# RWKV solve on 32x32 blocks in four array tiles, and six modulation blocks of each layer at another place

## The chip, the cores and the metric

The kernel runs on one core of one Trainium2 chip. The metric is device time in microseconds (us). Three runs of the kernel before took 1097.0, 1099.38 and 1100.24 us; the median is 1099.38.

## What is computed

The program is a decoder trunk of two layers on 256 positions and 1024 channels in float32. Each layer modulates a normed input with vectors `mod = silu(c) @ w_mod + b_mod`, projects it, and mixes it in three branches (a gated linear recurrence, differential attention, RWKV-7), which are merged by sigmoid gates; a gated MLP follows. The change touches two things: how the RWKV branch is solved, and when the modulation vectors are summed. For each of 8 heads RWKV is this recurrence:

```python
state = (state * w_t[:, :, None, :] + sa[..., None] * b_t[:, :, None, :]
         + v_t[..., None] * k_t[:, :, None, :])      # sa = state a_t
return state, jnp.einsum("bhvk,bhk->bhv", state, r_t)
```

The kernel cuts the 256 positions into 4 chunks of 64. Inside a chunk the recurrence is a linear system with a unit triangular 64x64 matrix, one for each of the 8 heads and 4 chunks, so 32 matrices in a layer. Between the chunks a state is handed on (the state chain).

## The kernel before, in words

Every engine runs a program of its own, in order, and the engines wait on each other's semaphores. Nothing plans the order: it is written out by hand.

**TensorE (PE).** Large products take weights in two parts (high and low, fp32r) and make three matmuls of each (`passes`, L1784 to L1786, and `token_unit`, L1973 to L1979). The gates and the merge weights of the branches are such products with 512 columns, cut into 36 weight chunks per layer. They depend on little, so they serve as filling: `fill(point)` issues the next `FILL[point]` of these matmuls wherever PE would otherwise wait for another engine. What is not used as filling is issued afterwards in one piece (`fill_some(12 * NCHUNK)`).

**The solve** (`STEPS`, `solve_steps`). It inverts the 32 triangular matrices by doubling: blocks of 2, then 4, 8, 16, 32 and 64, so five levels behind the first. The products are plain float32, and each shows as two matmul records and two weight loads in the trace. `chunk_products` (L2075) makes the matrices: K against KK ("ak"), KK against AB ("n") and AB against KK ("nt", the transposed form), each 32 products of 64x64. In them four array tiles are in use, since both the 64 rows of the head's half and the 64 columns of the chunk's half change. A level is two steps, "m" and "x", each done for `par` 0 and 1: `block_products` (L2084) makes 16 products of 64x64 per `par`, on the two diagonal tiles of the array. VectorE reads each result with a mask ("m", L1519) or adds it ("x", L1525), and after "x" it turns both matrices in blocks of 32 (L1529). Behind each step PE issues 8 matmuls of filling (6 behind the last). `Mm`, `Nm`, `Tm` and `TTm` hold 16 blocks of 64x64 each. The first level of all, with blocks of two, is made by `blocks_of_two` (L1491, L1515) on identities that ScalarE writes (L874, L875).

**Behind the solve** come the products with its result (L2125, L2132), the read products (L2075, L2149) and the state chain over 4 chunks: PE (L2166 to L2180) and VectorE (L1544 to L1554) in turn, with 4 matmuls of filling at a time, and one weight chunk's low part (L1350) by VectorE after each state.

**Modulation.** w_mod is read in blocks of 128x1024 (512 KB). VectorE adds each block to an accumulator (`mod_block`, L1112 for the first of 8 and L1115 for the others); `mod_beside(n)` takes the next n blocks at the place where it stands. Eight blocks make a vector, which PE then sums over partitions (`mod_sum`, L1743: a wait on `mod_used` for the eighth block, then 8 small matmuls), and VectorE reads (`mod_vector`). GpSimd (POOL) issues the loads into two buffers (`mod_blocks`, L560), each when the block two before it was used; between them it does the low parts of nine weight chunks (L586) and the state factors and merges (L594 to L607). SP issues the weight loads `pair(g)` of 1 MB into four buffers. ScalarE makes the high parts (`act_chunks`, L778).

## Time and profile before

| what | value |
|---|---|
| three runs | 1097.0 to 1100.24 us, median 1099.38 |
| the profiled execution | 1098.47 us |
| its span, first to last instruction | 1096.7 us |
| granted TensorE clock, mean | 0.992 |
| PE busy, VectorE busy, ScalarE busy | 98%, 77%, 53% of the span |
| DMA | 214.81 MB, mean 196 GB/s |

The span is 1.8 us shorter than the execution's own time, and this execution is 0.9 us below the median. PE is TensorE with its matmuls, PEld its weight loads. "Busy" of PE counts pipelined matmuls, so it says that PE is occupied and not that it is at its peak. "issue" as a releaser is time in which nothing that the profile shows held the engine. A clock of 1.0 is 2.4 GHz and one of 0.5 is 1.2 GHz.

### The profile page before, as it was taken

How to read it: one execution, taken by the hardware profiler on the slowest of the kernel's cores; microseconds unless marked ns; L12 is line 12 of the kernel's file. 1: busy time of each engine (PE TensorE's matmuls, PEld its weight loads, DVE VectorE, ACT ScalarE, POOL GpSimd, SP SyncE). 2: the span in 40 equal slices, each digit the busy share in tenths (PEclk: the TensorE clock that was granted, in tenths of full speed). 3: DMA queues.
4: the chain of work that ended last, by engine and by line, in shares of the span. 5: the costliest groups of instructions: out<-in, count | busy, mean ns of one | idle time of the engine just before them, and what ended most of it. 6: DMA issues, size and time to landing. Idle time of an engine off the chain costs nothing.

```text
span 1096.7 us, 23323 instructions
## 1 busy us (share of the span) xinstructions
PE 1075.3 (98%) x9660; PEld 989.9 (90%) x9660; DVE 845.3 (77%) x1245; ACT 582.7 (53%) x894; POOL 125.8 (11%) x142
## 2 busy tenths in 40 slices
PE   8999999899999999999999999999999999999997
PEld 7889988787789999999989999878887999999997
DVE  4798998686578798987758899977755878888763
ACT  2266567532364666663355575683227466666533
POOL 0100000056002000001120000002640200000001
PEclk8999999999999999999999999999999999999999
DMA  9946455443156567667854546361615465555651
GB/s 378 342 172 217 178 172 225 180 154 139 42 208 235 188 233 245 218 234 292 311 189 167 206 157 223 144 229 60 232 59 192 154 244 184 186 191 191 222 201 39
DMA packets 41460, 214.81 MB, mean 196 GB/s; under 512 B 7936, under 2 KB 8320, under 8 KB 22048
## 3 DMA queue, kind: packets, MB, share of 16 engines
q1 hardware_dynamic: 29856, 171.65, 42.8%
q0 software_dynamic: 11520, 41.95, 10.8%
q8 instruction: 64, 1.05, 0.4%
q14 instruction: 20, 0.16, 0.0%
HBM read 212.01 MB, written 1.05 MB: 194 GB/s over the span
## 4 chain that ended last, share of the span: by engine, by line
PE 93%; DVE 4%; DMA 2%; issue 1%; ACT 1%; DVEq 0%; ACTq 0%
PE ps L1786 18%; PE ps L1784 17%; PE ps L1785 17%; PE ps L1975 6%; PE ps L1979 6%; PE ps L1973 6%; PE ps L1804 5%; PE ps L2084 2%; DMA mring<-wmod_dram 2%; PE ps L1743 1%; DVE macc L1115 1%; PE ps L2256 1%; PE ps L2075 1%; PE ps L1761 1%; PE ps L2000 1%
## 5 line engine op out<-in xcount | busy, mean ns | idle before, releaser
L965 ACT ACTIVATE WH<-ring 128x1024 fp32r<-128x1024 f32 x144 | 151.9, 1060 | 164.9 <-PE ps L1786 157.2
L1634 DVE TENSOR_TENSOR WLO<-ring,WH 128x1024 fp32r<-128x1024 f32 x144 | 175.8, 1234 | 70.0 <-ACT WH L965 70.0
L1786 PE MATMUL ps<-HH,WLO 128*128 128x256 f32 x736 | 208.1, 283 | 0.0
L1785 PE MATMUL ps<-HL,WH 128*128 128x256 f32 x736 | 206.6, 281 | 0.0
L1784 PE MATMUL ps<-HH,WH 128*128 128x256 f32 x736 | 205.0, 279 | 0.0
L1786 PEld LDWEIGHTS ps<-HH,WLO 128*128 128x128 f32 x736 | 138.7, 188 | 0.0
L1784 PEld LDWEIGHTS ps<-HH,WH 128*128 128x128 f32 x736 | 138.5, 188 | 0.0
L1785 PEld LDWEIGHTS ps<-HL,WH 128*128 128x128 f32 x736 | 138.0, 188 | 0.0
L560 POOL DMA_DIRECT2D mring<-wmod_dram x80 | 43.4, 542 | 763.2 <-DVE macc L1115 456.5
L1115 DVE SCALAR_TENSOR_TENSOR macc<-mring,sm,macc 128x1024 f32<-128x1024 f32 x70 | 96.5, 1378 | 16.4 <-DMA mring<-wmod_dram 14.4
L1786 PE MATMUL ps<-GH,WLO 128*128 128x256 f32 x384 | 108.3, 282 | 0.0
L1784 PE MATMUL ps<-GH,WH 128*128 128x256 f32 x384 | 108.2, 282 | 0.0
L1785 PE MATMUL ps<-GL,WH 128*128 128x256 f32 x384 | 107.9, 281 | 0.0
L1786 PE MATMUL ps<-HG,RLO 128*128 128x256 f32 x384 | 107.9, 281 | 0.0
L1662 DVE SCALAR_TENSOR_TENSOR TK<-ps,PR,TK 128x255 f32<-128x255 f32 x192 | 79.1, 475 | 0.0
L1979 PE MATMUL ps<-RLO,HG 128*128 128x512 f32 x192 | 77.7, 405 | 0.0
L1786 PEld LDWEIGHTS ps<-GH,WLO 128*128 128x128 f32 x384 | 73.7, 192 | 0.0
L1786 PEld LDWEIGHTS ps<-HG,RLO 128*128 128x128 f32 x384 | 72.5, 189 | 0.0
L1785 PEld LDWEIGHTS ps<-GL,WH 128*128 128x128 f32 x384 | 72.2, 188 | 0.0
L1784 PEld LDWEIGHTS ps<-GH,WH 128*128 128x128 f32 x384 | 72.1, 188 | 0.0
L778 ACT ACTIVATE WC<-ring 128x1024 fp32r<-128x1024 f32 x36 | 37.8, 1055 | 62.3 <-PE ps L1975 33.1
L1784 PE MATMUL ps<-HG,WCR 128*128 128x256 f32 x208 | 58.8, 283 | 0.0
(404 smaller groups left out, 2552.7 us busy)
## 6 DMA issues: line engine op xcount, KB each, us to landing
ring<-wmain_dram SPq DMA_DIRECT2D x150, 1024.0 KB, 4.9
mring<-wmod_dram POOLq DMA_DIRECT2D x80, 512.0 KB, 5.0
G<-wmod_dram SPq DMA_DIRECT2D x3, 1024.0 KB, 10.0
R<-wmod_dram SPq DMA_DIRECT2D x3, 1024.0 KB, 17.7
TK<-wmod_dram SPq DMA_DIRECT2D x2, 1024.0 KB, 20.5
X<-x_t_dram SPq DMA_DIRECT2D x1, 1024.0 KB, 5.8
y_dram<-H SPq DMA_DIRECT2D x4, 256.0 KB, 2.1
SW<-small_dram SPq DMA_DIRECT2D x1, 512.0 KB, 13.6
```

The lines of the kernel that those rows point to most:

```text
L560: pool.dma_start(mring[:, n % 2, :], wmod[mod_row(n)]).then_inc(s_m[n % 2], 16)
L965: A(WH[:, n % 2, part], ring[:, b, part], ACT.Copy).then_inc(hi_ready, 1)
L1115: V.scalar_tensor_tensor(macc[:, u % 2, :], block, sm[:, CSIL + kt:CSIL + kt + 1], macc[:, u % 2, :], ALU.mult, ALU.add).then_inc(mod_used, 1)
L1634: V.tensor_tensor(WLO[:, n % 2, part], ring[:, b, part], WH[:, n % 2, part].bitcast(F32), ALU.subtract).then_inc(lo_ready, 1)
L1662: ins = V.scalar_tensor_tensor(UB[:, q % 2, t, d:S], duo(b)[:, t, 0:S - d], PR[:, l, bass.ds(j + (COL["fw"] + 48 * (2 - d)), 1)], UB[:, q ...
L1784: MM(out, w_high[:, at], high, start=start, stop=False, skip_group_check=True)
L1785: MM(out, w_high[:, at], low, start=False, stop=False, skip_group_check=True)
L1786: return MM(out, w_low[:, at], high, start=False, stop=stop, skip_group_check=True)
L1804: last = MM(ps[:, g % 4, m * S:(m + 1) * S], w_of(g, m, i), rhs[:, i, :], start=(i == 0), stop=(i == KT - 1))
L1973: MM(ps[:, b, :], high[:, tk], w_high, start=(k == 0), stop=False, skip_group_check=True)
L1975: i = MM(ps[:, b, :], low[:, tk], w_high, start=False, stop=False, skip_group_check=True)
L1979: i = MM(ps[:, b, :], high[:, tk], w_low, start=False, stop=(k == nk - 1), skip_group_check=True)
```

## The change

- The first four levels (blocks up to 32) work on the 32x32 diagonal blocks alone. A step has 32 products of 32x32 per `par` where it had 16 of 64x64, on four diagonal array tiles where it used two. The operands `Nn`, `Tn`, `TTn` and `Mn` have 256 elements per partition and `par` where they had 512, so VectorE's reads, adds and turns are half as long.
- The last level ("m" and "x" with v = 4) joins two 32x32 halves: "m" has 16 products per `par` on two tiles, "x" 32 on four, half of which only copy a block with the identity. VectorE copies the results, and one more operation writes the left half of `TTm`.
- "n" is made as 64 products with 64 rows and 32 columns (`narrow_products`), "nt" falls away, and in its place come 32 such products ("off"), which ScalarE reads.
- `blocks_of_two` falls away; two masks, two adds of the identity and two turns on VectorE take its place, and ScalarE no longer writes identities.
- Six calls' worth of modulation blocks leave the projections of each layer. One goes behind the solve, and five into the state chain. In layer 0 the eighth block of the first vector stands behind weight chunk 16, ahead of `mod_vector(6 * l + 2)`. GpSimd's loads are shifted to fit.
- SP loads the masks in 12 transfers where it needed 4.
- `FILL` is as before.

```diff
-(M_LOW, M_UP, M_UPI, M_L1, M_U1, M_U2, M_U4, M_U8, M_U16, M_U32, M_ID) = range(11)
...
+(M_UP, M_UPI, M_U32) = range(3)
+(N_LOW, N_UP, N_UPI, N_L1, N_U1, N_U2, N_U4, N_U8, N_U16, N_ID) = range(10)
+Q = 32
...
-LEVELS = [M_U2, M_U4, M_U8, M_U16, M_U32]
+LEVELS = [N_U2, N_U4, N_U8, N_U16, None]
+LAST = len(LEVELS) - 1
...
-    steps = [("ak", 0, 0, 4), ("ak", 1, 0, 5), ("n", 0, 0, 6), ("n", 1, 0, 7), ("nt", 0, 0, 4), ("nt", 1, 0, 5)]
+    steps = [("ak", 0, 0, 4), ("ak", 1, 0, 5), ("n", 0, 0, 6), ("n", 1, 0, 7), ("off", 0, 0, 4), ("off", 1, 0, 5)]
...
+def tiles_used(kind, v):
+
+    return {"ak": 1, "n": 4, "off": 2, "m": 2 if v == LAST else 4, "x": 4}[kind]
+
+
+SOLVED = [int(n) for n in np.cumsum([tiles_used(k, v) for k, _, v, _ in STEPS])]
...
-        TTm, Nm, Tm, Mm = mats(0, 4), mats(4, 8), mats(8, 12), mats(12, 16)
+        def narrow_mats(a):
+            return R[:, a:a + 2, :].rearrange("p a b -> p (a b)").rearrange("p (g m s) -> p g m s", g=2, s=Q)
+
+        TTm, Mm = mats(0, 4), mats(12, 16)
+        Nn, No, Tn, TTn, Mn = [narrow_mats(a) for a in (4, 6, 8, 10, 12)]
...
@@ -521,9 +555,14 @@
                 if l == 0:
                     for half in (0, 1):
                         rows = slice(64 * half, 64 * half + 64)
-                        sp.dma_start(CM[rows, 0:NCOMP - 1, :], consts[rows, AT_MASKS:AT_MASKS + (NCOMP - 1) * P]
+                        sp.dma_start(CM[rows, M_UP:M_UPI + 1, :], consts[rows, AT_UP:AT_UP + 2 * P]
                                      .rearrange("p (n s) -> p n s", s=P)[:, :, 64 * half:64 * half + 64]).then_inc(s_masks, 16)
-                        sp.dma_start(CM[rows, M_ID, :], consts[rows, 64 * half:64 * half + 64]).then_inc(s_masks, 16)
+                        sp.dma_start(CM[rows, M_U32, :], consts[rows, AT_U32 + 64 * half:AT_U32 + 64 * half + 64]).then_inc(s_masks, 16)
+                    for g in range(4):
+                        rows = slice(Q * g, Q * g + Q)
+                        sp.dma_start(CN[rows, N_LOW:N_ID, :], consts[rows, AT_MASKS:AT_MASKS + N_ID * P]
+                                     .rearrange("p (n s) -> p n s", s=P)[:, :, Q * g:Q * g + Q]).then_inc(s_masks, 16)
+                        sp.dma_start(CN[rows, N_ID, :], consts[rows, Q * g:Q * g + Q]).then_inc(s_masks, 16)
...
-                m1 = m0 + 16
-                mod_blocks(m0 + 2, m1)
...
                     if i < 7:
-                        mod_blocks(m1 + i, m1 + i + 1)
+                        mod_blocks(m0 + 10 + i, m0 + 11 + i)
...
-                mod_blocks(m1 + 7, m1 + 8)
+                mod_blocks(m0 + 17, m0 + 24)
...
-                act.wait_ge(s_masks, 64)
-                A(TTm.rearrange("p g m s -> p (g m) s"), over(small_mask(M_ID), 16), ACT.Copy).then_inc(i_ready, 1)
-                A(Tm.rearrange("p g m s -> p (g m) s"), over(small_mask(M_ID), 16), ACT.Copy).then_inc(i_ready, 1)
...
+                for par in range(2):
+                    act.wait_ge(t_mm, SOLVED[-1] * l + products_until("off", par))
+                    A(No[:, par], narrow(4 + par), ACT.Copy).then_inc(off_ready, 1)
...
-                mod_beside(2)
...
-                if l:
-                    mod_beside(2)
...
-                    mod_beside(2)
...
-                    if b == 1 or b == 3:
+                    if b == 3:
                         mod_beside(2)
...
                 dve_chunks(16, 17)
+                mod_beside(0 if l else 2)
                 mod_vector(6 * l + 2)
-                mod_beside(0 if l else 2)
...
-                dve.wait_ge(s_masks, 64)
...
                 for n, (kind, par, v, b) in enumerate(STEPS):
+                    if kind == "off":
+                        continue
                     dve.wait_ge(t_mm, mm0 + SOLVED[n])
...
                     elif kind == "n":
-                        V.tensor_tensor(Nm[:, par], oct(b), over(small_mask(M_LOW), 8), ALU.mult).then_inc(t_ev, 1)
-                    elif kind == "nt":
-
-                        blocks_of_two(par, oct(b), M_U1, 1).then_inc(t_ev, 1)
+                        V.tensor_tensor(Tn[:, par], narrow(b), over(narrow_mask(N_L1), 8), ALU.mult).then_inc(t_ev, 1)
+                        V.tensor_tensor(Nn[:, par], narrow(b), over(narrow_mask(N_LOW), 8), ALU.mult).then_inc(t_ev, 1)
                         if par:
                             for p2 in range(2):
-                                dve.wait_ge(t_ev, base + step_no("n", p2, 0) + 1)
-                                blocks_of_two(2 + p2, Nm[:, p2], M_L1, 0).then_inc(step, tick(n_step))
-                            dve.wait_ge(i_ready, 2 * (l + 1))
-                            dve.wait_ge(t_ev, base + n + 1)
+                                dve.wait_ge(t_ev, base + reads_until("begin", p2))
+                                V.tensor_tensor(Tn[:, p2], Tn[:, p2], over(narrow_mask(N_ID), 8), ALU.add).then_inc(step, tick(n_step))
                             for p2 in range(2):
-                                for at, T_, odd in ((p2, TTm[:, p2], 1), (2 + p2, Tm[:, p2], 0)):
-                                    if at >= 2:
-                                        dve.wait_ge(step, n_step[0] - 1 + p2)
...
-                                                    E[:, at, :].rearrange("p (j n) -> p j n", j=8), ALU.add).then_inc(t_init, 1)
+                                dve.wait_ge(step, n_step[0] - 1 + p2)
+                                V.transpose(flat(TTn[:, p2]), flat(Tn[:, p2])).then_inc(t_init, 1)
                             dve_chunks(18, 19)
                     elif kind == "m":
-                        V.tensor_tensor(Mm[:, par], oct(b), over(small_mask(LEVELS[v]), 8), ALU.mult).then_inc(t_ev, 1)
+                        if v < LAST:
+                            V.tensor_tensor(Mn[:, par], narrow(b), over(narrow_mask(LEVELS[v]), 8), ALU.mult).then_inc(t_ev, 1)
+                        else:
+                            V.tensor_copy(Mn[:, par], narrow(b)).then_inc(t_ev, 1)
                         if par == 1 and v == 0:
                             branch_low(1, YBL[:, :, :], YB[:, :, :], YH[:, :, :])
-                        elif par == 1 and v < 4:
+                        elif par == 1:
                             mod_beside(1)
+                    elif v < LAST:
+                        V.tensor_tensor(TTn[:, par], TTn[:, par], narrow(b), ALU.add).then_inc(t_ev, 1)
+                        if par == 1:
+                            for p2 in range(2):
+                                dve.wait_ge(t_ev, base + reads_until("x", p2, v))
+                                V.transpose(flat(Tn[:, p2]), flat(TTn[:, p2])).then_inc(t_turned, 1)
+                            if v == LAST - 1:
+                                V.tensor_scalar(TTm[:, :, :, 0:Q].rearrange("p g m s -> p (g m) s"), TTn.rearrange("p g m s -> p (g m) s"),
+                                                small_mask(M_U32)[:, CH - 1:CH], None, ALU.mult).then_inc(t_ev, 1)
+                                gated(2)
+                            else:
+                                mod_beside(1)
                     else:
-                        V.tensor_tensor(TTm[:, par], TTm[:, par], oct(b), ALU.add).then_inc(t_ev, 1)
-                        if par == 1 and v < len(LEVELS) - 1:
-                            for p2 in range(2):
-                                dve.wait_ge(t_ev, base + step_no("x", p2, v) + 1)
-                                V.transpose(flat(Tm[:, p2]), flat(TTm[:, p2])).then_inc(t_turned, 1)
-                            if v == 3:
-                                gated(2)
-                            mod_beside(1)
-
+                        V.tensor_copy(TTm[:, par, :, Q:CH], narrow(b)).then_inc(t_ev, 1)
+
+                mod_beside(1)
...
                     if c:
                         dve.wait_ge(u_mm, 3 * l + c)
                         V.tensor_tensor(WY[rows, tt, :], ps[rows, 4, :], WY[rows, tt, :], ALU.add).then_inc(u_ready, 1)
+                        mod_beside(1 if c < NCH - 1 else 2)
...
-                        if c == 1:
+                        if c:
                             mod_beside(1)
...
-                def block_products(b, a, bb, done):
+                def narrow_products(b0, tiles_, done):
 
                     for m in range(8):
-                        for c in range(2):
-                            last = MM(ps[halves[c], b, m * 64:(m + 1) * 64], a[halves[c], m, :], bb[halves[c], m, :], start=True, stop=True)
+                        tt, j = divmod(m, 4)
+                        for par in range(2):
+                            for g, ga_, gb in tiles_:
+                                rows, cols = slice(tt * P + Q * ga_, tt * P + Q * ga_ + Q), slice(tt * P + Q * gb, tt * P + Q * gb + Q)
+                                last = MM(ps[quarters[g], b0 + par, m * Q:(m + 1) * Q], KK[halves[par], j, rows], AB[halves[par], j, cols],
+                                          start=True, stop=True)
+                                if m == 7:
+                                    last.then_inc(done, 1)
+
+                def block_products(b, pairs_, done):
+
+                    for m in range(8):
+                        for g, a, bb in pairs_:
+                            last = MM(ps[quarters[g], b, m * Q:(m + 1) * Q], a[:, m, :], bb if len(bb.shape) == 2 else bb[:, m, :],
+                                      start=True, stop=True)
                             if m == 7:
                                 last.then_inc(done, 1)
 
                 pe.wait_ge(tk_ev, 8 * l + 8)
                 chunk_products(4, K_, KK, t_mm)
...
-                chunk_products(6, KK, AB, t_mm)
-                pe.wait_ge(t_ev, base + 2)
-                chunk_products(4, AB, KK, t_mm)
-
-                pe.wait_ge(t_ev, base + 4)
+                narrow_products(6, [(g, g, g) for g in range(4)], t_mm)
+                pe.wait_ge(t_ev, base + reads_until("ak", 1))
+                narrow_products(4, [(1, 1, 0), (3, 3, 2)], t_mm)
...
                         if v == 0:
-                            pe.wait_ge(t_init, 4 * l + 2 * par + 2)
+                            pe.wait_ge(t_init, 2 * l + par + 1)
                             pe.wait_ge(w1_ev, 2 * (l + 1))
                         else:
-                            pe.wait_ge(t_ev, base + step_no("x", par, v - 1) + 1)
-                        block_products(b, Nm[:, par], TTm[:, par], t_mm)
+                            pe.wait_ge(t_ev, base + reads_until("x", par, v - 1))
+                        if v < LAST:
+                            block_products(b, [(g, Nn[quarters[g], par], TTn[quarters[g], par]) for g in range(4)], t_mm)
+                        else:
+                            block_products(b, [(g - 1, No[quarters[g], par], TTn[quarters[g], par]) for g in (1, 3)], t_mm)
                     else:
-                        pe.wait_ge(t_ev, base + step_no("m", par, v) + 1)
+                        pe.wait_ge(t_ev, base + reads_until("m", par, v))
                         if v:
                             pe.wait_ge(t_turned, 8 * l + 2 * (v - 1) + par + 1)
-                        block_products(b, Tm[:, par], Mm[:, par], t_mm)
+                        else:
+                            pe.wait_ge(off_ready, 2 * (l + 1))
+                        block_products(b, [(g, Tn[quarters[g], par], narrow_mask(N_ID)[quarters[g], :] if v == LAST and g % 2
+                                            else Mn[quarters[g], par]) for g in range(4)], t_mm)
```

## Rows read from the trace of the kernel before

**Rows 1.** The page of the kernel before: its span and the busy time of each engine.

```profile
span 1096.7 us, 23323 instructions
...
PE 1075.3 (98%) x9660; PEld 989.9 (90%) x9660; DVE 845.3 (77%) x1245; ACT 582.7 (53%) x894; POOL 125.8 (11%) x142
```

**Rows 2.** The chain of work that ended last, by engine (part 4 of the page).

```profile
PE 93%; DVE 4%; DMA 2%; issue 1%; ACT 1%; DVEq 0%; ACTq 0%
```

**Rows 3.** Waits of PE in the whole run: waiter, releaser, us in total, times, longest.

```profile
PE ps L2075 <- issue: 2.1, 1, 2.1
...
PE ps L1784 <- DVE RLO L1191: 0.9, 1, 0.9
```

**Rows 4.** Busy time by window: length, PE, PEld, DVE, ACT, POOL, clock, DMA share, GB/s.

```profile
209.47:273.30 63.83, 59.24 (x1317) 49.77 (x1316) 45.48 (x60) 17.97 (x24) 30.86 (x22) 0.97 0.37 137
745.22:803.80 58.58, 57.37 (x1318) 48.02 (x1317) 45.45 (x60) 17.96 (x24) 29.15 (x21) 1.00 0.38 137
...
214.61:218.20 3.59, 3.59 (x99) 3.59 (x100) 1.80 (x6) 0.10 (x1) 0.00 (x0) 0.54 0.02 5
```

**Rows 5.** Timeline, layer 0: start us, length us, engine, line, operation, count.

```profile
209.47 1.02 PEld L2075 LDWEIGHTS ps<-KK,ZS 64*64 64x64 f32 x64 [0.35 <-issue]
...
220.98 1.94 PEld L2084 LDWEIGHTS ps<-R 64*64 64x64 f32 x64 [0.37 <-issue]
...
225.05 1.94 PEld L2084 LDWEIGHTS ps<-R 64*64 64x64 f32 x64 [0.36 <-issue]
```

**Rows 6.** Timeline of PE around its two waits for issue, layer 0.

```profile
212.10 0.44 PE L2075 MATMUL ps<-KK,AB 64*64 64x64 f32 x11 [0.53 <-DVE R L1499]
...
214.61 1.65 PE L2075 MATMUL ps<-KK,AB 64*64 64x64 f32 x51 [2.07 <-issue]
...
266.44 1.16 PE L2075 MATMUL ps<-ZS 64*64 64x64 f32 x64
...
270.50 0.68 PE L2149 MATMUL ps<-R,TK 64*64 64x64 f32 x29
272.58 0.80 PE L2149 MATMUL ps<-R,TK 64*64 64x64 f32 x35 [1.40 <-issue]
```

**Rows 7.** DMA queue of instructions, 209.47 to 273.3: packets, MB, share of 16 engines.

```profile
q8 instruction: 10, 0.16, 1.0%
```

**Rows 8.** The same queue in the window 212.1 to 212.3.

```profile
q8 instruction: 1, 0.02, 30.1%
```

**Rows 9.** The same queue in the window 215.6 to 215.8.

```profile
q8 instruction: 1, 0.02, 35.8%
```

**Rows 10.** DMA queue of the weights, 266.7 to 270.1.

```profile
q1 hardware_dynamic: 135, 0.98, 70.9%
```

**Rows 11.** Groups of VectorE in layer 0, 209.4 to 265: shapes, count, busy us, mean ns.

```profile
L1115 DVE SCALAR_TENSOR_TENSOR macc<-mring,sm,macc 128x1024 f32<-128x1024 f32 x6 | 11.1, 1846 | 1.8 <-DMA mring<-wmod_dram 1.8
...
L1519 DVE TENSOR_TENSOR R<-ps,CM 128x512 f32<-128x512 f32 x10 | 6.6, 685 | 0.6 <-PE ps L2084 0.5
...
L1491 DVE TENSOR_TENSOR E<-ps,CM 128x256 f32<-128x256 f32 x2 | 0.8, 420 | 3.2 <-PE ps L2075 3.2
```

**Rows 12.** Timeline of PE at the third modulation sum, layer 0.

```profile
199.46 1.02 PE L1743 MATMUL ps<-sm,macc 128*128 128x1 f32 x8 [0.38 <-issue]
```

**Rows 13.** Timeline of VectorE behind it, layer 0.

```profile
201.20 1.23 DVE L1350 TENSOR_TENSOR RLO<-ring,WC 128x1024 fp32r<-128x1024 f32 x1 [0.76 <-ACT WC L778]
...
202.42 2.67 DVE L1115 SCALAR_TENSOR_TENSOR macc<-mring,sm,macc 128x1024 f32<-128x1024 f32 x2
```

**Rows 14.** DMA issue of GpSimd in the window 197.2 to 197.6: count, KB, us to landing.

```profile
mring<-wmod_dram POOLq DMA_DIRECT2D x1, 512.0 KB, 5.5
```

**Rows 15.** Timeline of VectorE in the state chain, layer 0.

```profile
290.01 1.22 DVE L1350 TENSOR_TENSOR RLO<-ring,WC 128x1024 fp32r<-128x1024 f32 x1
291.27 0.69 DVE L1544 TENSOR_TENSOR WY<-ps,WY 64x512 f32<-64x512 f32 x1
296.16 1.29 DVE L1564 TENSOR_TENSOR KK<-AB,GG 128x512 f32<-128x512 f32 x2 [4.19 <-ACT AB L913]
```

51 lines of the change are left out of this document (32 added, 19 removed).

## The prediction

> **What bounds the kernel now.** I read the page first, then the chain of waits, then PE's own waits, and only then the stage that changes. PE is busy for 98% of the span [rows 1] and carries 93% of the chain that ended last [rows 2], so the time falls by what PE loses in work or waits, and by little else. The waits outside the changed stage are small: 0.9 us for VectorE at one half pair is the largest that it names there [rows 3]. VectorE at 77% has room, and the projections, which give up twelve modulation blocks, had almost nothing to win from it.
>
> I take the stage from the first "ak" product to the first product of the state chain. It lasts 63.83 us in layer 0 and 58.58 us in layer 1, with the same 1317 and 1318 matmul records [rows 4]. The reader should ask why the same work takes 5.2 us more in layer 0. Two waits for "issue" answer it, 2.07 and 1.40 us [rows 6], with a stretch of 3.59 us behind the first at a mean clock of 0.54 [rows 4]. At full clock the work of that stretch takes 3.59 x 0.54 = 1.9 us, so the lower clock cost 1.7 us. The sum is 5.2.
>
> **What "issue" was.** In the stage a DMA queue of instructions brings 10 packets, 0.16 MB [rows 7], for 1317 + 1316 = 2633 instructions of PE [rows 4], 263 to a packet; I take 256. The first wait ends 22 instructions into "nt" (11 records and their loads), right behind the 256 of "ak" and "n". The second is 2304, or 9 x 256, later by my count of the stage's order. So PE stood at the end of a packet both times. The packet that ended the first wait was moved between 212.1 and 212.3, took 0.301 x 16 x 0.2 = 0.96 us [rows 8], and PE went on at 214.61, about 1.4 us behind its end. A packet seems to be asked for when PE enters the one before. Counted back 256 instructions, that was at 209.6, so 5.0 us passed; for the second wait it was near 267.0 (37 records into the products at 266.44 [rows 6]), so 5.6 us. In the second case 0.98 MB of weights moved in between [rows 10]. After the first wait nothing else moved: PE entered at 214.61, the next packet started near 215.7 and took 0.358 x 16 x 0.2 = 1.15 us [rows 9], which with the 1.4 us makes 3.6 us. So 256 instructions cost at least 3.6 us on a quiet DMA and about 5.3 us on a loaded one. The step of before hides that: 128 + 16 instructions in 225.05 - 220.98 = 4.07 us [rows 5] is 7.2 us for 256.
>
> **PE's products.** Two tiles give 64 records of 64 columns in 1.94 us; four tiles give 64 in 1.02 us [rows 5]. The change runs 128 records of 32 columns on four tiles in every step. No row shows a 32x32 tile. If time goes with columns, they take 1.02 us, at best 0.92 us less than now. If the pace of records is what four tiles show at 64 columns (15.9 ns), they take 2.04 us and nothing is won. I take 1.02, since the trace's halving from two to four tiles says that tiles and not records set the pace. The eight steps of the narrow levels and both of the last ("m" 64 records on two tiles, "x" 128 on four) save about 0.85 us each once the changeovers are left as they are. "n" at 128 records and "off" at 64 replace "n" and "nt" at no cost, since VectorE's reading of "n" sets the end there as before. That is 8.5 us a layer for PE alone.
>
> The Trainium skill, TensorE: Matmul & The Clock Gate, "Wait - 56ns, not 53.3ns?", speaks against even that: matmuls never start closer than about 25 ns, however few columns. By it a step's products take 128 x 25 = 3.2 us, 1.3 us more than now, and the forecast would be near 1130 us; it goes with the third rival. The 64 records in 1.02 us [rows 5] are closer than that, so the trace doesn't agree.
>
> **Instructions.** By my count a layer's stage goes from 1216 to 1856 product records; each has a weight load, and with 100 filling matmuls and their loads that is 2632 and 3912 instructions (the trace has 2633). So 15.3 packets are needed where there were 10.3. A step is now 256 + 16 instructions in 4.07 - 0.92 = 3.15 us, 3.0 us for 256: less than even the 3.6 us of a quiet DMA. **PE then waits at nearly every packet.** The mean delay: DMA share is 0.37 in this stage [rows 4], so 0.37 x 5.3 + 0.63 x 3.6 = 4.2 us, and the stage lasts 15.3 x 4.2 = 64.3 us. Against 63.83 and 58.58 that is +0.5 and +5.7 us. Waits of 2 us like the traced one let the clock fall, 1.7 us a time; much of it hides under the next packet's delay, so I count one net in each layer, less a little: +3.0.
>
> **VectorE.** An operation on 256 elements takes 0.42 us where 512 took 0.685 [rows 11]. An "x" step is four of them and a block, 4 x 0.42 + 1.85 = 3.5 us at most, an "m" step 2.7; the mean of 3.1 just fits under 3.15, and the filling covers single excesses. Cost 0; if it isn't covered, 0.4 us a pair of steps, 3 us in all. The turns, the extra `TTm` write, ScalarE's two short reads and SP's eight further mask loads (before a weight buffer that is needed tens of us later) cost 0: each ends inside filling, and without it 1 us each at most.
>
> **The moved blocks.** In layer 0 the eighth block of the first vector now stands behind chunk 16. PE's `mod_sum`, which started at 199.46 [rows 12], waits for it, with every turn of the operands queued behind. The block's load is issued at 197.3 and lands 5.5 us later [rows 14], at 202.8; the block takes 1.3 us [rows 13], so PE goes on at 204.1 at the earliest. At the latest it is where the two blocks end now, 202.42 + 2.67 = 205.1 [rows 13]. That is a wait of 4.6 to 5.6 us that no filling covers; I take 4.7, as the chunk before it comes earlier without the identities. It is longer than the wait that brought the clock down, so I add 1.7: **+6.4 us**. Layer 1 has two more blocks before this point and doesn't wait. In the chain the blocks fill pauses of VectorE. The one that pushes something is behind chunk 29 (290.01): the last "u" moves from 291.27 by 1.3 us [rows 15], and PE has state products and four filling matmuls, about 2 us, before it needs it. The last block waits for its load (two buffers) until about 297.6, and pushes the gain products from 296.16 [rows 15] by about 2.7 us, ahead of a pause for ScalarE's root. Cost 0; with a load slower by 3 us, 3 us a layer. The six blocks taken from the projections are worth at most the 0.9 us [rows 3], which I credit.
>
> **Sum:** 0.5 + 5.7 + 3.0 + 6.4 - 0.9 = +14.7 us on this execution's 1098.47, so 1113 us. The median of the runs is 0.9 us above that execution; I don't correct for it.
>
> **Rivals.**
> - Packets come as on a quiet DMA every time (waiting PE asks for fewer weights). The stage is 15.3 x 3.6 = 55.1 us: -8.7 and -3.5, with +6.4 and -0.9 a total of -6.7, 1092 us. For it: the waits themselves thin the traffic. Against: the modulation loads don't thin. Chance 0.2.
> - Instructions don't bind (more than one packet is asked for ahead). Then -8.5 in each layer, the 5.2 us of layer 0 gone too, +6.4 and -0.9: -16.7, 1082 us, clearly faster. It decides if 256 instructions arrive in under 3.0 us. Against it stand both traced waits at packet ends. Chance 0.2.
> - Records set the pace of the array, at 15.9 ns. The packets' delay is then 0.37 x 5.3 + 0.63 x 3.8 = 4.4 us and the stage 67 us: 1118 us. For it: no row shows more than four tiles' pace. Against: two tiles and four keep the same time per tile. Chance 0.08.
> - The gains and the wait in layer 0 cancel: within 0.3%. Chance 0.06.
>
> **The numbers.** The forecast case has 0.46, with 1104 to 1122 us for delays of 3.9 to 4.4 us and one clock fall more or less in each layer. A measurement of this kernel can tell about 0.3% from no change. Faster is both first rivals less their overlap with no change, 0.36; same 0.06; slower 0.58. The range from 1085 to 1122 leaves out most of the second rival and the top of the third; the forecast case alone is 1104 to 1122.
>
> **What would show it.** Each stage should hold 15 or 16 packets and about 3910 instructions; PE should wait for issue ten or more times in each, 1 to 3 us at a time, with a granted clock below 1 behind the longer ones; L1743 should start near 204 in layer 0, while layer 1's is unmoved against its stage. Products should show 64 records of 32 columns in about 0.5 us. A stage near 50 us without waits for issue would prove the packet argument wrong; no wait at L1743 would take 6.4 us from the sum.

## The result, and the profile after

The changed kernel takes 1122.14 us (median of 4 runs, 1119.22 to 1127.21) where the kernel before takes 1098.19 in the same measurement (1096.09 to 1100.24): a ratio of 1.0222, 95% interval 1.0184 to 1.0259, so 24 us slower. 1113 us were forecast, with a range from 1085 to 1122, so the result lies just above it. The profiled execution took 1122.23 us. Now and then an execution of any of these kernels is over 1.5% longer, at a lower clock; the ratios leave such executions out, the medians don't. Its page, against [rows 1, 2]:

```profile
span 1120.4 us, 25891 instructions
...
PE 1076.1 (96%) x10940; PEld 987.7 (88%) x10940; DVE 830.5 (74%) x1243; ACT 580.1 (52%) x894; POOL 125.3 (11%) x142
...
q8 instruction: 74, 1.21, 0.4%
...
PE 92%; DVE 3%; issue 3%; ACT 1%; POOL 1%; DMA 0%; DVEq 0%; ACTq 0%
```

PE is busy as long as before, 1076 us: what its cheaper products save, stretches at the lower clock take back. The span grew by 23.7 us, and 22.9 of them are time in which PE does nothing. "issue" has 3% of the chain where it had 1%. PE's waits in the whole run, against [rows 3]:

```profile
PE ps L2132 <- issue: 14.1, 10, 3.3
PE ps L1778 <- DVE macc L1153: 5.3, 1, 5.3
...
PE ps L2014 <- issue: 4.0, 1, 4.0
PE ps L2123 <- issue: 2.1, 2, 1.5
PE ps L2204 <- issue: 1.1, 1, 1.1
PE ps L2147 <- issue: 1.0, 1, 1.0
```

L2132 is the new block product (L2084 before), L1778 the modulation sum (L1743 before), L2014 filling, L2123 "n", L2147 the products of W, L2204 the last read product. The five lines for issue make 22.3 us, all of it between the first product set and the state chain of a layer. Windows (length, PE busy, clock, DMA share, GB/s): the two solves (here and below, a layer's stretch from the first product set to the state chain), against [rows 4], and the stretch around layer 0's modulation sum.

```profile
219.48:286.81 67.33, 55.85 (x1958) 0.92 0.35 120
760.26:827.27 67.01, 55.24 (x1957) 0.92 0.34 121
198.87:204.75 5.88, 0.54 (x3) 0.99 0.60 242
204.75:214.40 9.65, 9.65 (x39) 0.50 0.30 105
214.40:219.48 5.08, 5.08 (x34) 0.96 0.63 210
```

By the starts of the stages the 23.7 us are: 10.0 up to layer 0's first product set, 3.5 in its solve, 1.5 in the turns of layer 1, 8.4 in layer 1's solve, and 0.3 elsewhere. The state chain, into which blocks were moved, takes 22.46 us as before. Within a solve PE works 3.4 and 2.1 us less than before, and idles 11.5 and 11.8 us instead of 4.6 and 1.2. The granted clock is 0.50 for 9.65 us behind the wait of 5.34 us: the lower of its two levels, 1.2 instead of 2.4 GHz.

The waits for issue fall at fixed counts. Numbering PE's instructions from the run's start (matmuls, weight loads and the semaphore instructions between them), the eight waits of layer 0's solve come behind 2753, 3009, 4033, 4289, 4545, 5057, 5313 and 6337, and the seven of layer 1's behind 14065, 15089, 15601, 15857, 16369, 16625 and 16881. Within a layer all are multiples of 256 apart, give or take one. They last 0.2 to 4.0 us.

### The profile page after: what moved, and what is told of

Its sections match the earlier page's. It is cut to its first block, busy times and chain, and to the rows that moved or that the text cites. A ratio compares the mean times of both kernels' runs of the same rounds, so it can differ in the third digit from the quotient of the medians.

```text
span 1120.4 us, 25891 instructions
## 1 busy us (share of the span) xinstructions
PE 1076.1 (96%) x10940; PEld 987.7 (88%) x10940; DVE 830.5 (74%) x1243; ACT 580.1 (52%) x894; POOL 125.3 (11%) x142
## 3 DMA queue, kind: packets, MB, share of 16 engines
q0 software_dynamic: 11520, 41.95, 10.9%
q8 instruction: 74, 1.21, 0.4%
## 4 chain that ended last, share of the span: by engine, by line
PE 92%; DVE 3%; issue 3%; ACT 1%; POOL 1%; DMA 0%; DVEq 0%; ACTq 0%
PE ps L1821 17%; PE ps L1819 16%; PE ps L1820 16%; PE ps L2010 6%; PE ps L2014 6%; PE ps L2008 6%; PE ps L1839 5%; PE ps L2132 3%; PE ps L1778 2%; PE ps L2311 1%; PE ps L1796 1%; PE ps L2097 1%; PE ps L2035 1%; PE ps L1965 1%; DVE RLO L1620 1%
## 5 line engine op out<-in xcount | busy, mean ns | idle before, releaser
L2014 PE MATMUL ps<-RLO,HG 128*128 128x512 f32 x192 | 77.6, 404 | 0.0
L1819 PE MATMUL ps<-HG,WCR 128*128 128x256 f32 x208 | 58.8, 283 | 0.0
```

The costliest lines, as they stand in the source:

```text
L1819: MM(out, w_high[:, at], high, start=start, stop=False, skip_group_check=True)
L2014: i = MM(ps[:, b, :], high[:, tk], w_low, start=False, stop=(k == nk - 1), skip_group_check=True)
```

## The experiments

Each was run in turns with the kernel before. "The base" is the run `e5_early_eighth`. Table of the medians:

| run | us | ratio to before, 95% interval |
|---|---|---|
| e1_solve_only | 1120.4 | 1.0222, 1.0149 to 1.0295 |
| e2_moves_only | 1106.2 | 1.0075, 1.0052 to 1.0097 |
| e3_split | 1135.1 | 1.0333, 1.0271 to 1.0395 |
| e4_two_tiles | 1096.2 | 0.9977, 0.9947 to 1.0007 |
| e5_early_eighth | 1112.9 | 1.0139, 1.0091 to 1.0186 |
| e6_refill | 1128.5 | 1.0272, 1.0236 to 1.0308 |
| e7_before_refill | 1100.4 | 1.0029, 1.0011 to 1.0047 |
| e8_shift_l0 | 1101.1 | 1.0050, 1.0027 to 1.0072 |
| e9_covered | 1111.6 | 1.0161, 1.0109 to 1.0214 |
| e10_half_heads | 1097.5 | 0.9996, 0.9970 to 1.0022 |
| e11_spread | 1107.3 | 1.0098, 1.0065 to 1.0131 |
| e12_shift_six | 1100.1 | 1.0014, 0.9993 to 1.0035 |
| e13_fine | 1136.6 | 1.0361, 1.0257 to 1.0465 |
| e14_fine_n | 1128.4 | 1.0266, 1.0212 to 1.0320 |
| e15_before_fine | 1143.4 | 1.0431, 1.0383 to 1.0480 |

The windows quoted below are those of the two solves of a run (layer 0, layer 1), cut at the same two products as [rows 4]; their columns are those of [rows 4].

**The two halves of the change alone.** In `e1_solve_only` the six blocks of each layer stand where they stood; `e2_moves_only` is the opposite.

```
e1 (on after):  + mod_beside(2) in its old four places, - the mod_beside calls behind the solve and in the chain
                - mod_blocks(m0 + 2, m0 + 10)
                + mod_blocks(m0 + 2, m1)            (m1 = m0 + 16, and so on)
e2 (on before): the reverse of these lines, the solve untouched
```

> The changed kernel with all six moved modulation blocks of each layer back at their old places; the solve on 32x32 blocks stays. Theory A (two separate causes: in the solve, TensorE issues twice the instructions and these arrive in lots of 256 that can't be fetched faster than one in about 4 to 5 us; before the solve, a wait for the eighth block that layer 0 no longer has in time, and a half clock behind it): the wait of 5.3 us at the modulation sums and the half clock before the first product set are gone, the stretch from the first product set to the state chain stays near 67 us in layer 0 and in layer 1 (63.8 and 58.6 before): 1098 + 3.5 + 8.5 = about 1110 us. Theory B (the solve costs nothing by itself; what grew there are the blocks moved into it and a clock that the wait had lowered): stretches back to 64 and 59 us, about 1098 us, or less.

> The kernel before with only the six modulation blocks of each layer moved; its solve on 64x64 blocks stays. Theory A: VectorE's eighth block of layer 0 comes some 5 us after TensorE asks for it, the clock is at half for about 10 us behind this wait, and so the first product set begins about 10 us later than in the kernel before; from there on both solves take what they took before, 64 and 59 us: about 1098 + 10 + 1 (a like gap in layer 1) = 1108 to 1110 us. Theory B (the moves cost only because the solve was changed with them): about 1098 us. A third theory, that the moved blocks delay the state chain, would show in the stretch of the chain (22.4 us in both kernels so far).

The windows of e1, then those of e2:

```profile
207.77:280.97 73.20, 57.58 (x1957) 46.16 (x1956) 35.51 (x59) 18.61 (x26) 31.50 (x22) 0.88 0.35 121
754.56:825.36 70.80, 58.81 (x1957) 47.20 (x1956) 34.20 (x59) 18.73 (x26) 28.87 (x21) 0.86 0.32 115
```

```profile
217.86:277.28 59.42, 57.58 (x1317) 48.18 (x1316) 45.70 (x61) 17.96 (x24) 30.75 (x22) 1.00 0.38 135
750.91:809.36 58.45, 57.32 (x1317) 48.02 (x1317) 45.67 (x61) 17.96 (x24) 29.12 (x21) 1.00 0.38 138
```

Theory B is out: the solve is slow without any moved block, and by more than theory A gave (21 us where 12 were expected). Its solves are 5.9 and 3.8 us longer than the changed kernel's. In layer 0 most of that is idle time (15.6 us against 11.5), in layer 1 it is PE's work at a lower clock (58.8 us busy against 55.2, clock 0.86 against 0.92). e2 came out 7 us slower (8 by the ratio) where 10 to 12 were expected. Its first product set starts 8.4 us late, but its solve of layer 0 then takes 59.4 instead of 63.8 us: the wait of 2.1 us for issue [rows 3] isn't there (1.8 us of idle time in that solve instead of 4.6), and so neither is the half clock behind it [rows 4] (PE is busy 1.7 us less). The two halves add up to 28 us, the whole change to 24; the interval of e1 alone is 8 us to either side, so the difference says nothing.

**The eighth block of layer 0.** `e5_early_eighth` finishes it earlier; `e9_covered` leaves it late and puts work of PE ahead of the wait.

```
e5: -                    if b == 3:
    +                    if b == 3 or (b == 1 and l == 0):
                             mod_beside(2)
    -                mod_beside(0 if l else 2)
e9: +                        if l == 0:
    +                            fill_some(18)
                             mod_sum(6 * l + 2, lambda: fill_some(2))
    (18 taken from n == 2, n == 4, fill(7) and fill(LEVEL0 - 1) of layer 0)
```

> The changed kernel with layer 0's two late blocks (those at the first modulation step behind the derived values) back beside the second of the four query-key groups, so that all eight blocks stand before the modulation sums. Theory A: no wait at the sums of layer 0, no half clock before the first product set, and nothing else moves: 1122 - 10 = about 1112 us (5.3 us of wait and about 4.9 us of clock). If the clock falls for another reason than the wait, only 5 us come back: about 1117 us. If VectorE was the bound there and only carries the delay elsewhere, about 1122 us.

> The changed kernel with 18 projection products put ahead of layer 0's modulation sums (4.2 us of TensorE's work), taken from the six placed in the turns, the eight behind them and four of the eight behind the first products of W; VectorE's order is not touched, so the eighth block is as late as in the changed kernel. If the toll is the idle TensorE and the half clock behind it: the wait of 5.3 us shrinks to about 1 us, the clock stays at full for most of the turns, and the turns lose cover for ScalarE's copies (1 to 3 us): 1122 - 7 = about 1115 us. If the lateness itself is the toll (VectorE behind it sets what follows): 1120 us or more.

Both hit: e5 took 1112.9 us where 1112 were expected, e9 1111.6 (1116 by its ratio) where 1115 were. The intervals of both ratios touch that of the changed kernel, so the profiles have to carry it. In e5 the first product set starts at 209.02 us, as before and 10.5 us ahead of the changed kernel's. In e9's profile the sum starts at 204.57 us, as late as in the changed kernel (204.60), but PE arrives there working; the turns then begin at 206.85 us at a full clock:

```profile
204.57 1.05 PE L1778 MATMUL ps<-sm,macc 128*128 128x1 f32 x8
...
206.85 1.07 PE L2099 MATMUL ps<-C,KK 128*128 128x128 f32 x8
```

```profile
201.00:212.14 11.14, 10.11 (x72) 8.66 (x70) 3.56 (x4) 4.29 (x9) 1.05 (x2) 1.00 0.65 241
```

e9's first product set starts at 212.14 us, 7.3 us ahead of the changed kernel's. So the toll was PE's idleness and the clock behind it, not VectorE's lateness: 10 us together, in a kernel whose wait is 5.3 us. The rest of the loss, about 14 us in e5, is the solve. Its windows:

```profile
209.02:279.68 70.66, 54.17 (x1957) 43.40 (x1957) 37.56 (x60) 18.62 (x26) 30.42 (x22) 0.95 0.32 115
751.30:816.69 65.39, 53.99 (x1957) 43.89 (x1956) 37.38 (x60) 17.56 (x25) 29.23 (x21) 0.95 0.34 124
```

PE works 5.1 and 3.4 us less than in [rows 4], and idles 16.5 and 11.4 us. That is the change in one line: it saves PE up to 5 us of work a layer and takes 10 to 12 us of idle time for it.

**What the idle time is.** `e3_split` gives the kernel before the instruction count of the changed one; `e4_two_tiles` and `e10_half_heads` take half of the level products from the base.

```
e3 (on before): +  for w in range(2):
                       MM(ps[halves[c], b, m * 64 + 32 * w:...], a[halves[c], m, :], bb[halves[c], m, 32 * w:32 * w + 32])
e4 (on e5):     -  for g in range(4)]          +  for g in (0, 2)]      (levels 0 to 3)
e10 (on e5):    -  for m in range(8):          +  for m in range(0, 8, 2):   (levels 0 to 3)
```

> The kernel before, with each product of the five levels of its solve, 64x64 by 64x64, issued as two products of 32 columns: 1280 more instructions in each layer between the fifth set and the last, the same columns through the array, the same VectorE work, the same waits. Theory A (the supply of instructions in lots of 256 sets the pace): the stretch from the first product set to the chain rises by some 3 us in layer 0 and 6 to 8 us in layer 1, with gaps for issue at a fixed distance of 256 instructions: about 1098 + 10 = 1108 us. Theory C (the new solve is slow because of its small tiles, of switching among four of them, or of VectorE's copies): no more than about 1 to 2 us, since the additional products are short: 1099 us.

> The kernel of the run e5_early_eighth with the products of two of the four array tiles (the second and the fourth block) left out in the first four levels, so half of the inverse isn't computed: 1024 fewer TensorE instructions of the solve's products in each layer (instructions of weight loads counted), while VectorE's and the projections' work, the waits and their order stay. Theory A (the supply of instructions): with 128 instead of 256 instructions in a step, a lot lasts two steps, no gaps for issue are left in these levels, and the stretch falls from 70.7 and 65.4 us to about 54 us or less in both layers: 1112.9 - 28 = about 1085 us. Theory C (VectorE's steps or ScalarE's copies are the bound): the stretches stay near 65 us, about 1110 us. Theory D (two tiles in turn cost as much array time as four, only the switching counts): the products' busy time stays at 15 us a layer, and the gain is that of the gaps alone, about 1092 us.

> The kernel of the run e5_early_eighth with every second product group of the first four levels left out, in all four tiles (so half of the heads' inverses aren't computed, VectorE handling what stood there): again 1024 TensorE instructions fewer in each layer, this time with the four tiles in turn as in the changed kernel. Theory A (number of instructions): no gaps for issue at the levels' products, as in the run with two tiles, and the products' busy time is about 7.7 us a layer where that run had 12.5; VectorE's steps take over as the bound (they took 7.2 us of idle there), so about 1090 to 1096 us. Theory D (what costs is the passing among four tiles): gaps named issue stay at these products, half as many, and the time is near 1102 us.

The groups of level products in the whole runs of before, e3 and after, in this order (one fence each); then the first window of e3, and the first windows and the largest wait of e4 and of e10.

```profile
L2084 PE MATMUL ps<-R 64*64 64x64 f32 x1280 | 41.6, 220 | 1.2 <-DVE R L1519 1.2
```

```profile
L2085 PE MATMUL ps<-R 64*64 64x32 f32 x2560 | 78.9, 219 | 0.0
...
209.32:288.38 79.06, 76.34 (x1958) 67.24 (x1957) 42.40 (x60) 17.95 (x24) 30.43 (x22) 1.00 0.31 111
```

```profile
L2132 PE MATMUL ps<-R 32*32 32x32 f32 x2304 | 30.3, 198 | 10.8 <-issue 10.8
```

```profile
211.12:269.50 58.38, 51.18 (x1446) 41.36 (x1445) 44.95 (x60) 18.50 (x26) 31.03 (x22) 0.97 0.39 138
...
PE ps L2131 <- DVE R L1544: 5.1, 4, 2.4
```

```profile
209.51:269.76 60.25, 49.16 (x1445) 38.77 (x1444) 46.65 (x60) 18.62 (x26) 30.55 (x22) 0.94 0.37 133
...
PE ps L2131 <- DVE R L1552: 10.0, 6, 3.8
```

e3 missed by 27 us. Halving the columns didn't halve the price: 78.9 us for 2560 records is 30.8 ns a record, against 32.5 ns (41.6 / 1280) with 64 columns. On two tiles that is 62 and 65 ns per tile and record, nearly the same with half the columns. The changed kernel's 30.3 us for 2304 records are 13.2 ns in the mean, 53 ns per tile on four. (The mean holds pieces cut by waits, some at half clock, and the last level's on two tiles; a step without a wait takes 1.4 to 1.65 us for its 128 records, as the lines further down show.) So the price goes by the record, and the small blocks need nearly twice the records; 41.6 us of level products became 30.3 + 2.9, not half. The Trainium skill, TensorEngine Tiling (Array Packing), "Instruction Overhead", has this: a matmul has about 60 cycles of overhead, and one with a single free column takes as long as one with 60. The trace agrees for 32 columns against 64; no run here shows the overhead by itself. The same run answers the question it was made for from the other side: with 2860 instructions from the first product of W to the first behind the solve (2732 in the changed kernel), but each pair of them slower, it has no wait for issue at its level products at all. It isn't the number of instructions but their pace.

e4 and e10 say the same: with half the instructions, on two tiles or on four, no wait for issue is left at the level products, and PE waits for VectorE there instead (in the base VectorE's steps were hidden). Because of this new bound e4 is 11 us above what theory A gave it, and e10 1.5 us above its upper end. Passing among four tiles is no cause (theory D): e10 does it and has no gap for issue there. A perfect supply would leave less to win than the idle time: VectorE's steps stand right behind.

The Trainium skill, Advanced Engine Details and Errata, "ISA Cache", speaks of lines of 16 KB, 256 instructions each, and only two of them, though it also gives TensorE 128 KB. The trace agrees with the two lines: 74 packets of 1.21 MB in all, gaps 256 instructions apart, and one packet held ahead. It shows nothing of a larger store. How long a packet takes is only in the traces. Where PE found nothing at two borders (places between packets) in a row it went on 3.5, 5.0, 4.1, 6.2, 4.8, 4.7 and 6.0 us apart in layer 0 of the base.

The changed kernel's trace shows what makes one packet later than the next. Three borders in a row in layer 0, the last one empty for 3.3 us:

```profile
241.71 1.06 PE L2132 MATMUL ps<-R 32*32 32x32 f32 x89 [0.16 <-issue]
245.55 1.13 PE L2132 MATMUL ps<-R 32*32 32x32 f32 x97 [0.34 <-issue]
252.33 1.70 PE L2132 MATMUL ps<-R 32*32 32x32 f32 x107 [3.30 <-issue]
```

All that the DMA queues moved from 241.71 to 242.85, then from 245.55 to 249.90, and the instruction packet in what follows, 249.90 to 252.33:

```profile
q0 software_dynamic: 3, 0.01, 1.8%
```

```profile
q1 hardware_dynamic: 166, 1.26, 80.4%
q0 software_dynamic: 33, 0.07, 4.3%
```

```profile
q8 instruction: 1, 0.02, 2.5%
```

PE crosses a border at 241.71 us while the DMA is quiet, and the next packet starts at 242.93, 1.2 us later. It crosses the next one at 245.55 while weights are loaded, and the packet starts only at 249.97, 4.4 us later. The packets themselves take 0.9 to 1.5 us in either case, and each of the 15 waits in the two solves ends 1.2 to 1.6 us behind the end of its packet. Of the packets of these two solves all that started 2 us or more behind the crossing had the DMA engines about half busy or more in between; with the DMA quiet none took more than 1.2 us. So a lot (the 256 instructions of a packet) costs 3.7 or 3.8 us in layer 0 beside a quiet DMA, and 6.0 and 6.8 us beside weight loads. No run moved the weight loads to test this.

**More filling in the solve, or the same filling spread.** A step of the base is 256 product instructions (128 records and their loads), one passage to the filling and 8 filling matmuls of 0.23 us. Two of its steps in a row that hold no wait, layer 1:

```profile
764.04 1.39 PE L2131 MATMUL ps<-R 32*32 32x32 f32 x128
...
767.41 1.39 PE L2131 MATMUL ps<-R 32*32 32x32 f32 x128
```

That is 3.4 us for 272 instructions, 3.65 us at most in such steps. (The expectations below say 3.4 us for the products and 5.25 us for the step; that counted the weight loads as if they were records. The step asks for a lot every 3.2 to 3.4 us and not every 5, which is why it waits so often.)

`e6_refill` puts 24 more fillings of each layer there, `e7_before_refill` does it to the kernel before; `e11_spread` splits the filling of a step in two, `e13_fine` puts one behind every second group of products, `e14_fine_n` also between those of "n", `e15_before_fine` is the control on before.

```
e6, e7: -FILL = [8, 32, 48, 32, 36, 8, 20, 8] + [8] + [8, 8] * 4 + [8, 6]
        +FILL = [8, 32, 48, 32, 28, 8, 20, 8] + [8] + [10, 10] * 4 + [11, 11]
e11:    -                    if par == 1:
        -                        fill(LEVEL0 + 2 * v + ("m", "x").index(kind))
        +                    fill_some(n_fill // 2 if par == 0 else n_fill - n_fill // 2)
e13, e15, in block_products:
        +                        if m % 2 and rest[0]:
        +                            rest[0] -= 1
        +                            fill_some(1)
```

> The kernel of the run e5_early_eighth (the changed kernel with all eight blocks of layer 0 early), with 24 more projection products between the steps of each layer's solve: 10 behind each step and 11 behind the last two, where 8 and 6 stood; 8 of them are taken from the stretch ahead of the solve and 16 from behind the state chain, so their number stays. Theory A (TensorE idles in the solve because its instructions come in lots of 256, each some 4 to 6 us behind the last, while it runs 256 of them in 3.4 us plus 8 projection products of 0.23 us): the 24 products, 5.6 us per layer, go into time in which it idles now (16.5 us of layer 0's 70.7 and 11.4 us of layer 1's 65.4). The stretch from the first product set to the chain grows by less than the 5.6 us, what lies around it falls by 5.6 us, and the kernel gains up to 5.6 us a layer: 1103 to 1109 us, against 1112.9. Theory C (VectorE's steps are the bound of the solve): TensorE's idle time would be filled too, so this run tells A from C by the count at which the gaps fall alone. Theory D (the idle time is in TensorE itself, a cost of switching among tiles): the stretch grows by the whole 5.6 us, about 1113 us.

> The kernel before with the same 24 projection products of each layer moved into its solve. Its two stretches had 4.6 and 1.2 us in which TensorE did nothing, so there is little to fill: Theory A gives 1095 to 1099 us. More than 3 us won here would say that the placing of the projection products was a lever of its own, not one that the small blocks opened.

> The kernel of the run e5_early_eighth with the projection products inside the solve split: half of them between the products of the two halves of a step, half behind, where all stood behind. Nothing is added or taken away. Theory A (lots of 256 instructions, one asked for ahead): a step is 256 + 16 instructions, so any lot holds the same mix wherever it begins, and the idle time for issue stays at some 25 us in the run: 1110 to 1116 us. A rival (the burst of 256 product instructions in a row empties what has come, and the 8 projection products give it time to fill up again): split in two, the bursts are half as long and the idle time falls by several us, to about 1105 us or less.

> The kernel of the run e5_early_eighth with the same number of projection products in the solve, now one behind every second group of products (32 TensorE instructions) instead of 8 in a row behind 256. Theory A (only the mean rate counts: 272 instructions in 5.25 us of work against lots of 256 that come in about 5 us): no better than when all stood in a row; TensorE idles for issue some 25 us in the run, about 1113 us. Theory F (bursts count: 256 product instructions in a row run in 3.4 us, faster than a lot comes, and the credit from the slow projection products can't be stored, since only one lot is held ahead; the split in two of the run before gave back about 5 us): the idle time falls again, to 10 us or less in the run, and the time to about 1100 to 1105 us.

> As e13_fine, and also four of the eight projection products ahead of the levels put between the products of n. Theory F: the idle time at n (3.3 to 3.9 us in the run) falls too, by 2 to 3 us against e13_fine. Theory A: no change against e13_fine.

> The kernel before with its projection products spread in the same way within the steps of the solve. It has 128 + 16 instructions in a step, and hardly an idle moment for issue in the levels. Both theories: 1096 to 1100 us, unless VectorE's results come later because TensorE's products of a step now end later; then up to 3 us more.

e6: windows of its two solves and of the stretch behind layer 0's state chain, and two waits.

```profile
210.09:286.61 76.52, 63.25 (x1981) 51.01 (x1980) 36.12 (x60) 19.79 (x27) 28.98 (x21) 0.91 0.34 120
760.54:830.39 69.85, 59.91 (x1981) 48.51 (x1980) 36.42 (x60) 19.68 (x27) 28.96 (x21) 0.95 0.36 131
309.10:368.58 59.48, 53.98 (x337) 47.61 (x336) 42.77 (x57) 33.59 (x46) 7.48 (x7) 0.94 0.49 183
...
PE ps L2131 <- issue: 12.5, 8, 4.4
PE ps L2007 <- DVE RLO L1384: 9.0, 2, 4.9
```

A miss by 20 us. The idle time in the solves fell from 27.9 to 23.2 us, less than half of the 11.2 us of work put in, and with the lower clock of layer 0 (0.91, base 0.95) the two solves grew by 5.9 and 4.5 us, nearly by all that was put in. Taking 16 fillings from behind the chain uncovered a new wait there, 4.9 and 4.1 us for VectorE's low parts (L1384), with a fall of the clock behind it (0.94): that stretch grew by 3.9 us instead of shrinking by 3.7. In e7 the same edit cost 0.3%, 1 to 3 us above what was expected: filling was no lever of its own.

e11 changed only the place. Its windows:

```profile
209.64:276.33 66.69, 58.22 (x1957) 44.44 (x1956) 36.28 (x60) 18.61 (x26) 30.75 (x22) 0.92 0.35 122
749.89:816.49 66.60, 57.79 (x1958) 44.16 (x1957) 36.20 (x60) 17.55 (x25) 29.20 (x21) 0.92 0.35 122
```

The idle time is 17.3 us instead of 27.9, the busy time 7.8 us more, the two solves 2.8 us shorter. The median, 1107.3 us, lies between the two theories. It is 5.6 us below the base's, but the two ratios come from two measurements and their intervals overlap: a small gain, likely and not certain. In e13 the waits for issue at the level products are gone, as theory F said, yet the kernel is 24 us slower than the base by the medians and 16 us by the spans of the profiles (1127.1 and 1110.9 us). Both theories missed. Its timeline says why:

```profile
230.19 0.33 PE L2131 MATMUL ps<-R 32*32 32x32 f32 x16
230.45 0.50 PE L2013 MATMUL ps<-RLO,HG 128*128 128x512 f32 x1
230.88 0.33 PE L2131 MATMUL ps<-R 32*32 32x32 f32 x16
```

Sixteen records and one filling take 0.69 us from start to start (230.19 to 230.88), so the eight of a step take 5.5 us where the base's step, the same work with one passage instead of eight, takes 3.4. So each passage from tiles to the whole array and back costs 0.30 us. In e15 it is 0.34 us: eight periods of 0.81 us (230.21 to 231.02), 6.5 us, less the 4.07 us of the step before [rows 5], over seven.

```profile
230.21 0.45 PE L2084 MATMUL ps<-R 64*64 64x64 f32 x8
230.59 0.50 PE L1973 MATMUL ps<-WCG,HG 128*128 128x512 f32 x1
231.02 0.45 PE L2084 MATMUL ps<-R 64*64 64x64 f32 x8
```

That cost explains e15's 46 us, where nothing to 3 us were expected: 68 more passages a layer at 0.34 us are 23 us. In e13 136 passages at 0.30 us are 41 us; PE is busy 37 us more in its two solves (72.9 and 72.7 us against 54.2 and 54.0) and idles 21 us less. Of e11's 7.8 us of busy time, 20 more passages are some 6. e14's profile is as long as e13's (spans of 1127.4 and 1127.1 us), the intervals overlap, and its wait for issue at "n" is 0.7 instead of 2.0 us: a small hit at most.

Did the even spreading stop the waits in e13, or only the slower work? The pace decides it in favour of the second. PE works through 256 instructions in 3.2 to 3.4 us in the base, 5.6 us in e3 (two starts of its products, 5.93 us and 272 instructions apart, stand below) and 5.2 us in e13 (34 in 0.69 us); before, 7.2. The first waits at the level products, the other three don't.

```profile
230.11 3.94 PE L2085 MATMUL ps<-R 64*64 64x32 f32 x128
...
236.04 3.94 PE L2085 MATMUL ps<-R 64*64 64x32 f32 x128
```

And where the supply binds, the stretch behind the first product set takes 4.6 to 5.2 us per 256 instructions (2732 in 51.3 and 51.1 us in after, 53.0 and 49.2 in the base, 55.7 and 54.5 in e1, twice 50.3 in e11), nearly whatever work lies between. So theory F isn't needed, though no run rules it out; theory A stands with its pace corrected, and spreading pays only as far as the passages it adds fall into time that is idle anyway.

**Where the lot's border falls.** `e8_shift_l0` moves 8 fillings of layer 0 in the kernel before, `e12_shift_six` 6.

```
e8:  -                fill(4)
     +                fill_some(FILL[4] if l else FILL[4] - 8)
     +                        if l == 0 and (v, kind) == (4, "x"):
     +                            fill_some(8)
```

> The kernel before with 8 projection products of layer 0 moved from just ahead of the turns to the last step of the solve; nothing else changes, layer 1 not at all. These are 16 TensorE instructions, so that the first product set, the densest stretch (382 instructions in 3.8 us when nothing stops it), begins 16 instructions earlier in its lot of 256. Theory A (a lot is asked for when the one before it begins, and takes 4 to 5 us to come): in the kernel before the set takes 6.5 us in layer 0, where it begins at the 172nd instruction of a lot, and 3.8 us in layer 1, where it begins at the 84th; at the 156th its stop shrinks to under 1 us, and the half clock behind it goes too. Seen already in the run e7_before_refill, which had the same start in layer 0: idle time of 0.6 us in the stretch and a full clock, but a slower run of the turns (9.4 instead of 7.8 us). So here 4.0 us of idle and 1.8 us of clock less, 1.6 us more in the turns: 1098 - 4 = about 1094 us. A rival (the stop is a wait on data that the trace calls issue): it stays, 1098 us.

> The run e8_shift_l0 with 6 instead of 8 projection products moved. That run's stop in the first product set had gone as Theory A said (3.8 instead of 6.5 us), yet it was 0.5% slower and not faster. The question is where the time went. Theory E: the clock falls once in this part of layer 0 whatever one does, and without the stop it falls later and for longer (in that profile behind the first products of the state chain, 37.4 us instead of 22.4): then here too the first set takes 3.8 us, and a half clock is seen between 270 and 320 us, with a time of 1098 to 1103 us. Theory A alone: no such fall, about 1094 us.

The local forecast held in both: the first product set takes 3.82 us where it took 6.48, and the 2.1 us for issue [rows 3] are gone. The total didn't follow: 1101.1 us in e8, where 1094 were expected, and 1100.1 in e12, ratios of 1.0050 and 1.0014 to before. e12's profiled execution shows the full effect, 1094.4 us and a clock of 1.00 in the solve:

```profile
207.13:270.22 63.09, 59.09 (x1323) 49.32 (x1322) 47.34 (x60) 18.07 (x24) 31.13 (x22) 1.00 0.41 144
```

But six other runs took 1096 to 1102 us at mean clocks of 0.989 to 0.995. The kernel before does the same from run to run: 1093.1 us at 0.996 and 1100.5 at 0.989. So it seems that a fall of the clock that was taken away in one place comes in most runs in another, as theory E says, and its time was right. But the fall itself isn't shown: e12's profile, the only one of it, has none between 270 and 320 us, and e8's, where the state chain of layer 0 ran at 0.54, is of an execution of 1117.4 us, while e8's median is 1101.1. Where the clock falls in the usual run, and whether e8's few us come from that, stays open.

## Why the prediction was right or wrong

- **What binds: right.** PE's instructions in packets of 256, asked for one ahead, bind the solve. The waits stand at the packets' borders, 14 and 15 packets came in the two solves, and the waits number eight and seven, of 0.2 to 4.0 us, where ten or more in each, of 1 to 3 us, were forecast. e3, e4 and e10 show that it is the supply.
- **The stage: 64.3 us and 1.5 us of clock forecast, 67.3 and 67.0 measured.** The mean delay came out at 67.2 / 15.3 = 4.4 us, not 4.2: together 2.7 us of the miss. The formula (packets times a delay) holds, but its delay is no constant: e1 and the base run the same instructions in 65.4 to 73.2 us. The quiet delay of 3.6 us was right (3.7 and 3.8 measured), the loaded one of 5.3 us low (6.0 and 6.8 in layer 0).
- **The wait in layer 0: 4.7 us forecast, 5.3 measured,** for the block and at the place named.
- **The step that failed: "It is longer than the wait that brought the clock down, so I add 1.7".** It is the term for the moved blocks, +6.4 us. The lower clock lasted 9.65 us at 0.50 and cost 4.8 us. The 1.7 us were the price behind a wait of 2.1 us, and a wait two and a half times as long was given the same price though the sentence itself says that it is longer. The whole term was 10.0, not 6.4, by the start of the first product set; e5 gave back 10.5 us there and e9 7.3 (the median of e5 says 9.3, that of e9 10.5). With this one term right the forecast is 1117 us.
- **Left out: 1.5 us in the turns of layer 1,** where the granted clock is 0.50 from 751 to 754 us. PE's only idle time just ahead of it is 0.4 us at 748.6 us, which the kernel before and the base have too without such a fall, so its cause is open. And **0.9 us credited** to the projections that never came: the wait of 0.9 us at the half pair is there as before.
- **PE's products: wrong, and without effect.** 1.02 us for 128 records of 32 columns were taken, the other end 2.04. They take 1.4 to 1.65, and a step 3.4 to 3.65 where 3.15 was taken. The assumption that time goes with columns failed by e3. The third rival (records set the pace, at 15.9 ns) was off by as much to the other side; that its 1118 us stood nearest is luck: its mean delay of 4.4 us came from the array's pace, the measured one from packets beside weight loads. Since instructions bound, the price cost nothing here. Its rule from the Trainium skill, TensorE: Matmul & The Clock Gate, "Wait - 56ns, not 53.3ns?", would have given, as an estimate, 3.2 us for 128 records on four tiles. The trace shows about half of that, so it doesn't hold across tiles; per tile the records are 43 ns apart in the mean (4 x 1.39 us / 128), and nothing speaks against it.
- **State chain, VectorE, ScalarE, SP at nothing: right.** 22.46 against 22.45 us in layer 0. But VectorE's cover is thin, as e4 and e10 show.

Sum: 23.7 us against 14.7: 3.6 from the wait and its clock, 1.5 and 1.2 from the two solves, 1.5 from the turns of layer 1, 0.9 from the credit, 0.3 rest.

No version with the small blocks that computes the whole inverse beats the kernel before; e11 is the best of them, 1.0% above.

## What to carry to other kernels

Count a change's TensorE instructions as well as its columns: smaller blocks double the records, a record of 32 columns cost nearly what one of 64 did, and a dense burst outruns the supply of instructions, which then shows as "issue" at fixed counts. Look at what else the DMA moves then: a packet asked for beside weight loads came up to 3 us later. Filling covers this only if it slows the whole mix below the supply's pace, and it mustn't be spread finely, since each passage between tiles and the whole array has its own price. Price a wait of TensorE with the stretch at the lower clock behind it, and read that price from a wait of the same length, or take it away by putting work of TensorE ahead of the wait.

## What the runs showed of the hardware

- A float32 record of 64 rows costs 30.8 ns with 32 columns and 32.5 ns with 64, two tiles in turn; one of 32 rows and columns, four in turn, costs 10.9 ns in a step without a wait (1.39 us / 128) and 13.2 ns in the mean of the run.
- A passage between small tiles and 128x512 products and back costs 0.30 us (32x32, e13) to 0.34 us (64x64, e15).
- With TensorE waiting at border after border, lots of 256 instructions came 3.5 to 6.8 us apart. The next packet started 1.0 to 1.2 us behind the crossing of a border with the DMA quiet (241.71 us: 1.2), and up to 4.4 us behind it while weights were loaded (245.55 us); it took 0.9 to 1.5 us, and TensorE went on 1.2 to 1.6 us behind its end.
- Behind 5.3 us without work TensorE ran 9.65 us at a granted clock of 0.50 (1.2 GHz). With work put ahead of the same event the clock stayed at 1.00.
